# Opening of a two-layer kernel: a third output block in the wide banks, sums of squares by stationary squares, inputs from two queues

## The reference

```
h = rmsnorm(x, g_pre_mix)          # x * rsqrt(mean(x*x) + eps) * g
z = h @ w_in                       # split into s5 input u, conv x/b/c, q, k, v, f, gates
s5_mixer(u, ...), short conv, forgetting attention on q, k, v with decay from f
out = x + rmsnorm((sum of gate * branch @ w_branch) @ w_out, g_post_mix)
```

## Time and profile before

| | |
|---|---|
| median of 3 runs | 3633.23 us (3633.01 to 3633.37) |
| the profiled execution | 3627.11 us, its span 3625.6 us |
| PE busy | 3472.5 us, 96% of the span |
| DVE, ACT, POOL busy | 39%, 24%, 25% |
| mean granted TensorE clock | 0.986 |
| DMA | 333.40 MB, 92 GB/s over the span |

### The profile page before, as it was taken

The page is one execution under the profiler, slowest core; times in us unless marked ns, Lnnn a source line. Parts: engine busy times, 40 slices in busy tenths (PEclk is TensorE's granted clock), DMA queues, the critical chain, the costliest instruction groups (busy, mean ns, idle before and its releaser), DMA issues. The chain is left out here.

```text
span 3625.6 us, 40637 instructions
## 1 busy us (share of the span) xinstructions
PE 3472.5 (96%) x16148; PEld 2802.7 (77%) x16148; DVE 1429.7 (39%) x1581; ACT 874.9 (24%) x1067; POOL 905.2 (25%) x455
## 2 busy tenths in 40 slices
PE   7999999998999999999999999899999899999997
PEld 5787788887876888888867877677777688888886
DVE  7733566554324121212244436553542521121123
ACT  3222222224332111111222222212342411111112
POOL 2211111112331222222421124131254222222224
PEclk9999999999999999999999999999999999999998
DMA  3535434215412111111234222113263211111113
GB/s 120 149 95 140 142 127 136 96 70 198 162 41 76 52 46 47 46 52 46 93 111 126 86 93 93 64 64 135 93 215 127 76 46 46 46 46 52 46 46 128
DMA packets 101600, 333.40 MB, mean 92 GB/s; under 512 B 11920, under 2 KB 21520, under 8 KB 101328
## 3 DMA queue, kind: packets, MB, share of 16 engines
q1 hardware_dynamic: 100000, 326.90, 27.3%
q10 hardware_dynamic: 1472, 4.72, 0.3%
HBM read 249.06 MB, written 85.52 MB: 92 GB/s over the span
## 5 line engine op out<-in xcount | busy, mean ns | idle before, releaser
L272 POOL TENSOR_TENSOR w_lo<-w_raw,w_hi 128x1024 fp32r<-128x1024 f32 (+1 forms) x305 | 691.9, 2272 | 2547.6 <-ACT w_hi L268 2547.3
L311 PE MATMUL pair<-act_hi,w_hi 128*128 128x512 f32 x2992 | 967.4, 404 | 13.8 <-issue 7.4
L311 PE MATMUL pair<-act_lo,w_hi 128*128 128x512 f32 x2992 | 943.4, 396 | 0.0
L311 PE MATMUL pair<-act_hi,w_lo 128*128 128x512 f32 x2992 | 942.2, 396 | 0.0
L311 PEld LDWEIGHTS pair<-act_lo,w_hi 128*128 128x128 f32 x2992 | 564.6, 189 | 138.2
L311 PEld LDWEIGHTS pair<-act_hi,w_lo 128*128 128x128 f32 x2992 | 563.4, 188 | 137.7
L311 PEld LDWEIGHTS pair<-act_hi,w_hi 128*128 128x128 f32 x2992 | 545.2, 189 | 133.9 <-issue 15.9
L268 ACT CAST w_hi<-w_raw 128x1024 fp32r<-128x1024 f32 x275 | 288.4, 1049 | 970.7 <-PE pair L311 911.3
L594 DVE TENSOR_TENSOR p<-pair,rs 128x1024 f32<-128x1024 f32 x100 | 122.3, 1223 | 410.9 <-PE pair L311 398.7
L1832 DVE TENSOR_TENSOR f2v<-pair,rs 128x1024 f32<-128x1024 f32 x42 | 51.5, 1225 | 346.5 <-PE pair L311 346.5
L311 PE MATMUL pair<-f1hl,w_hi 128*128 128x512 f32 x480 | 147.8, 389 | 0.0
(11 more groups left out here) (471 smaller groups left out, 3966.9 us busy)
## 6 DMA issues: line engine op xcount, KB each, us to landing
w_raw<-in_stream SPq DMA_DIRECT2D x276, 512.0 KB, 3.6
proj<-p SPq DMA_DIRECT2D x101, 512.0 KB, 2.6
m2g<-proj SPq DMA_DIRECT2D x32, 512.0 KB, 4.6
foxx<-proj SPq DMA_DIRECT2D x32, 256.0 KB, 5.7
m1g<-proj SPq DMA_DIRECT2D x16, 512.0 KB, 3.3
x<-f1y SPq DMA_DIRECT2D x16, 512.0 KB, 2.6
act_lo<-x SPq DMA_DIRECT2D x16, 512.0 KB, 6.7
n1x<-in_x ACTq DMA_DIRECT2D x8, 512.0 KB, 9.1
```

What stands on the lines that cost most here:

```text
L272: last = nc.gpsimd.tensor_tensor(wlo[:, slot, at:at + n], raw[:, slot, at:at + n], whi[:, slot, at:at + n].bitcast(F32), ALU.subtract)
L311: last = nc.tensor.matmul(out_pair[:, h * HALF:(h + 1) * HALF], wt, a[:, h * HALF:(h + 1) * HALF], start=k == 0 and n_pass == 0, stop=k == ...
```

## The change

It acts in the opening, and by it on what is left for the background.

- The two first weight units are fetched without the wait for `s_split`. The loads x0 to x3 stay with ACT, x4 to x7 go to SP, behind the weights. The three S5 constants go to SP, after tile 0.
- A third output block, U1, is made in the opening. Its weights come as a tensor of their own (`third`), loaded by SP, split by ACT (line 1002) and POOL (line 1003) after tile 0, and its products (line 979) go into `wide`, which `row_sums` no longer needs. Third(0) and third(1) stand behind tile 1, third(k) behind tile k.
- The column sums of the squares are taken by `half_sums` in two banks (line 451): the squares are stationary and a column of ones moves, and the sums come out with one token on a partition, so that neither the diagonal nor the reduction is needed. They stand ahead of the last tile, the root's two halves behind them, the spreading (line 473) behind the last tile of F and U0, and third(7) behind that.
- DVE evicts the third block (line 1970) into the buffer of x0, after the four half evictions, and SP stores it.
- The background has 50 blocks instead of 51. The `upto` marks in S5 are lowered by eight tiles.
- Slots, pairs and the buffers of `p` swap their roles from there on, since one unit less has gone through the stream.

```
     def fetch_unit(b, slot):
-        SP.wait_ge(s_split, b + 1)
+        if not (isinstance(b, int) and b < 2):
+            SP.wait_ge(s_split, b + 1)
...
-                arrived = [x_in_sem[k].mark(nc.scalar.dma_start(x[:, k, :], x_in[k])) for k in range(KT)]
-                s5_in.mark(nc.scalar.dma_start(bb[:, 0:2, :, :], t["s5_b"]))
-                s5_in.mark(nc.scalar.dma_start(cc[:], t["s5_c"]))
-                got = s5_in.mark(nc.scalar.dma_start(dg[:], t["s5_d"]))
-                first_split()
+                raw3, hi3, lo3 = (sb(at, "n1w" + n, [P, KT * P], dt) for n, dt in (("r", F32), ("h", F32R), ("l", F32R)))
+                raw3_in = store.mark(SP.dma_start(raw3[:], t["third"]))
+                arrived = [x_in_sem[k].mark((nc.scalar if k < 4 else SP).dma_start(x[:, k, :], x_in[k])) for k in range(KT)]
...
+                def third(k):
+
+                    for half in halves:
+                        for n_pass, (wt, a) in enumerate(((hi3, act_hi), (hi3, act_lo), (lo3, act_hi))):
+                            last = nc.tensor.matmul(wide[:, half], wt[:, k * P:(k + 1) * P], a[:, k, half],
+                                                    start=k == 0 and n_pass == 0, stop=k == KT - 1 and n_pass == 2)
+                    return last
...
+                    if k == 0:
+                        first_split()
...
+                    if k == KT - 1:
+                        sums = [half_sums(bank[h][:], squares[:, halves[h]], True, True, added[k]) for h in range(2)]
+                        roots = [half_root(h, bank[h][:], 1.0 / D, sums[h]) for h in range(2)]
                     PE.after(split)
                     for o in range(2):
                         for h in range(2):
                             first_two.tile(o, h, k)
+                    if k == 0:
+                        a = A.mark(A.after(raw3_in).copy(hi3[:], raw3[:]))
+                        third_ready = G.mark(G.after(a).tensor_tensor(lo3[:], raw3[:], hi3[:].bitcast(F32), ALU.subtract))
+                        for n in range(3):
+                            s5_in.mark(SP.dma_start((bb[:, 0:2, :, :], cc[:], dg[:])[n], (t["s5_b"], t["s5_c"], t["s5_d"])[n]))
+                        got = s5_in.last()
+                    if k == 1:
+                        PE.after(third_ready)
+                        third(0)
+                    if k == KT - 1:
+                        for h in range(2):
+                            spread = half_spread(h, bank[h][:], roots[h])
+                            rs_ready = A.mark(A.after(spread).copy(rs[:, halves[h]], bank[h][:]))
+                    if k:
+                        last = third(k)
                     if 0 < k < KT - 1:
                         for _ in range(3):
                             next(early, None)
-                spread_inv_sqrt(rs, 1.0 / D, row_sums(squares, 0, 1, added[KT - 1]), rows=True)
-                V.after(A.last())
-                for o, evict in enumerate(first_evicts):
+                third_done = PE.mark(last)
+                V.after(rs_ready)
+                for o, evict in enumerate(first_evicts[0:2]):
                     for h in range(2):
                         first_two.evicted(o, h, evict)
                 stored[F_], stored[U_] = outs[0].last(), outs[1].last()
+                stored[U_ + 1] = first_evicts[2](x[:, 0, :], third_done)
...
-            w.upto(KT + 2)
+            w.upto(2)
...
-            w.upto(3 * KT + 1)
+            w.upto(2 * KT + 1)
...
-        rows = rows[2:]
+        rows = rows[3:]
...
-            w.upto(15 * KT + 1)
+            w.upto(14 * KT + 1)
```

More of the change, by code:

```diff
@@ L973, in s5 @@
                 squares, added = sq[:, 0, :], {}
+                halves = [slice(h * HALF, (h + 1) * HALF) for h in range(2)]
+                def third(k):
[4 more added lines that the diff above has]
+                    return last
                 for k in range(KT):
@@ L1937, in evict_u_half, with evict_third @@
                 outs[o].mark(SP.dma_start(s5_u.rearrange("(n p) j m -> n p (j m)", p=P)[0], buf[:, o, :]))
+        def evict_third(staged, ready):
+            v = V.mark(V.after(ready).tensor_tensor(staged.rearrange("p (j m) -> p j m", j=T),
+                                                    wide[:].rearrange("p (m j) -> p j m", j=T),
+                                                    rs[:].rearrange("p (m j) -> p j m", j=T), ALU.mult))
+            SP.wait_ge(*v)
+            return store.mark(SP.dma_start(s5_u.rearrange("(n p) j m -> n p (j m)", p=P)[1], staged))
         first_two = TwoBlocks(KT, act_rhs)
         with Woven(products(0, used["units"], n, n, KT, act_rhs, evict), n * KT, 1) as w:
-            s5(first_two, (evict_row, evict_u_half), w, stored)
-            w.upto(15 * KT + 1)
+            s5(first_two, (evict_row, evict_u_half, evict_third), w, stored)
+            w.upto(14 * KT + 1)
             w.again(FOX_HEADS * 24 + 8, KT)
@@ L1950, in _build @@
                 ops.load(r, mixed1[r], into=8 + r if r < 4 else None, *{0: (weighed, A.last(), stores[1].last()), 9: (normalised, mixed_out)}.get(r, ()))
-            gates = [gates1[:, 0, :], gates1[:, 1, :], buf[:, 1, :]]
-            merging = merge(ops, proj1, GATE1, 3, "b_gate", gates, buf[:, 0, :], [rs[:], rs[:]],
-                            [(stored[GATE1 + 8 * br], outs[1].last()) for br in range(3)],
+            gates = [gates1[:, 0, :], gates1[:, 1, :], buf[:, 0, :]]
+            merging = merge(ops, proj1, GATE1, 3, "b_gate", gates, buf[:, 1, :], [rs[:], rs[:]],
+                            [(stored[GATE1 + 8 * br], outs[0].last()) for br in range(3)],
                             lambda: [s.last() for s in outs], {0: (8, 12)})
@@ L2025, in _stream @@
     conv = [w[row + n:row + n + 1] for n in range(4) for row in (X_, B_, C_)]
-    parts = [_tiles(f), w[U_:X_], w[Q_:F_], *conv, _tiles(w_in[:, n_f + FOX_HEADS:])]
+    parts = [_tiles(f), w[U_:U_ + 1], w[U_ + 2:X_], w[Q_:F_], *conv, _tiles(w_in[:, n_f + FOX_HEADS:])]
     wb = _tiles(x["w_branch"][0])
@@ L2082, in _lay_out @@
         "stream": _stream(x),
+        "third": _units(_tiles(x["w_in"][0][:, (U_ + 1) * P:(U_ + 2) * P]).reshape(KT, P, P))[0],
         "s5_b": by_pair(b), "s5_c": by_pair(c),
```

## The result

| | before | with the change |
|---|---|---|
| median | 3632.91 us (20 runs, 3627.01 to 3634.88) | 3638.2 us (20 runs, 3631.46 to 3641.87) |
| ratio to before | | 1.0017, 95% interval 1.0010 to 1.0024 |
| the profiled execution | 3627.11 us | 3638.36 us |

The change costs 5.3 us where a gain of 9.7 was forecast.

What follows compares the result with a forecast made beforehand. DVE was taken to bound the stretch before the first transposition of constants, PE nearly all the rest. Opening +0.3, background -11.2 and take-back +1.2 sum to -9.7 us: 3623.5 us from the median 3633.23, range 3619.5 to 3629.5.

Steps and rivals of the forecast that it cites:

- Start of PE: In the opening: earlier weight loads let PE start at 11.45 us instead of 14.41, bounds 10.8 and 12.1.
- PE through the opening: PE stays supplied, `act_lo` of tile 1 just ahead of 16.6; first eviction possible at 50.2 us instead of 51.99.
- rival C: DVE's 33.15 us stretch shortens as POOL's splits fall elsewhere, or the opening is PE-bound earlier: 3620.5 us; chance 0.12.
- From there to `fox`: From the first transposition of constants to `fox`: PE bound again with its order unchanged, slow matmuls as before; zero.
- The background, -11.2: 50 background blocks instead of 51: 48 matmuls fewer, one tile ahead of `fox` and seven in it, -11.2 us.
- take-back: In the attention: tiles gone lengthen waits and their moving pattern opens a few new ones, +1.2 us, bounds 0 and +5.
- The prediction's own sign of being wrong: In `fox`: the prediction is wrong if PE's waits there grow by more than 5 us.
- Rival D: In `fox`: gaps on PE lower the clock, once in each of eight heads, 33 us; total 3656 us; chance 0.03.
- Rival A: In `fox`: half of the eight missing tiles turn into waits, gain only 5.3 us: 3627.9 us; chance 0.15.
- B: In the opening: late weights make `act_lo` of tile 1 2 to 3 us late, never recovered: 3626.2 us; chance 0.09.
- E: The change doesn't do what it says; only the spare bank could be missing; chance 0.01.
- A rule on POOL and DVE: In the opening: DVE and POOL lock each other out on SBUF; the third block's split costs DVE up to 2.4 us.

Runs made afterwards that it cites:

- Experiment 2: Changed kernel, with `fox` preparing the next head one step later (n == 5 instead of 4): 3623.92 us, ratio 0.9973.
- experiment 1: Changed kernel, with the eight missing tiles taken out of the S5 mixer instead of the attention: 3624.95 us, ratio 0.9974.
- experiment 3: Kernel before, with eight more background tiles handed out ahead of the attention and so eight fewer in it: 3651.31 us, ratio 1.0052.
- experiments 5 to 8: 5: kernel before, POOL held for key split, 3632.74 us; 6: later preparation there, 3633.72; 7: experiments 1 and 2 together, 3624.6; 8: kernel before, loads and sums, 3628.75.
- the sums alone: Kernel before, with only the new sums by stationary squares ahead of the last tile: 3631.55 us, ratio 0.9997.
- the loads alone: Kernel before, with only the weights fetched without their wait and x loaded from two queues: 3626.54 us, ratio 0.9988.
- experiment 6: Kernel before, with the next head prepared one step later in `fox`: 3633.72 us, ratio 1.0004.

## Why the prediction was wrong

*Start of PE:* forecast 11.45, measured 11.37. Right.

*PE through the opening:* I had `act_lo` of tile 1 just ahead of 16.6; it came late by 1.20 us, at 17.38, with the sums at 44.75 instead of 43.2. First eviction 51.25 instead of 50.2, constants at 56.96 instead of 55.6, first transposition 89.38 instead of 88.8. The term was +0.3 with bounds of -0.9 and +1.5. At the constants it measured +1.7, just outside; DVE's stretch from there to the transposition is 0.8 us shorter than before (rival C's mechanism, in small), so that +0.9 arrives. The number is within its bounds, partly by luck.

*From there to `fox`:* forecast zero, measured -1.3. The first transposition of `fox` comes 1.8 us earlier, and 1.4 of it is the one tile less ahead of it. The forecast took the slow matmuls behind PE's idle time as unchanged; with the change the clock is 1.00 and 0.83 from 80 to 100 us instead of 0.92 and 0.74.

*The background, -11.2:* stands. Experiment 2 shows it: with waits of 11.1 us in `fox` against 10.3, the stage takes 10.9 us less than before.

***The step that failed* is the take-back,** "the pattern of one or two tiles moves along the whole stage and will open a few new ones", +1.2 with bounds of 0 and +5. It measured 17.7 us: 12.1 of waits, 3.6 to 5.1 of clock, and a rest that no row names. The prediction's own sign of being wrong, waits in `fox` growing by more than 5 us, came. The bound came from the waits that the stage already had the earlier trace rows, and this is the wrong yardstick: shifting a pattern doesn't only lengthen old waits, it brings work of other engines, which comes at each block's end, into steps where it was not. What would have shown it was at hand. I compared the order of PE in `fox`, where one tile was missing, and not that of DVE, where an eviction had changed places in seven heads. And the waits of 0.6 us for line 821 said which step has no slack. A DVE instruction of 1.22 us ahead of it, and the split of the keys stretched beside POOL, for which I had a size from the opening (2.36 and 2.82 us for an operation of 1.28), would have given 1 to 2.5 us per head (an estimate from these rows).

*Rival D* had the mechanism, gaps in `fox` and then the clock, "from about three such gaps on". There were four, with three falls. Its price, one fall in each of eight heads, was too high, and its chance of 0.03 too low. *Rival A* had only waits as long as the tiles taken out. *B* came in small: the third weights are cast at 12.73, forecast about 11.2, and `act_lo` of tile 1 comes 1.2 us late instead of 2 to 3. *C* gave the 0.8 us above and not 3. *E* is out: the third block is made.

*A rule on POOL and DVE.* The rows at 477 us show the two engines one behind the other. POOL starts at 477.28 while DVE still has line 715 to 478.35, and takes 3.31 us where it takes 2.37 alone; line 716 starts at 478.38, and ends 1.1 us after POOL's end at 480.59. The rule of the Trainium skill that I weighed (SBUF — State Buffer, section "Who interferes with whom": the one that starts second blocks until the first is done) fits this within 0.15 us: POOL would end at 478.35 + 2.37 = 480.72 and line 716 at 480.59 + 1.22 = 481.81, where the rows have 480.59 and 481.68. I applied it only to the opening. There it did cost something: `act_lo` of tile 1 takes 2.47 us at 14.86, beside the split of the third weights, and at the 1.28 us of the undisturbed tiles it would have been done at 16.14, where PE waits until 17.38.

## What to carry to other kernels

When a change alters how much background work is spread over a periodic foreground, compare the order on every engine that the end of a block triggers, not only on the one that does the background work. Find the foreground's step without slack from its waits, however small, and ask what now falls into it. Work removed from the background can be more than lost again (11.2 us gained, 17.7 lost), and where the block ends fall can be set by hand: eight tiles given out earlier or later decided 13 us in the changed kernel (experiment 1) and 18 in the one before (experiment 3).

## What was not expected of the hardware

- The granted clock fell behind waits of 2.91 to 2.99 us three times, and not behind one of 2.87. The length alone doesn't decide it. In experiment 3 the same four waits stand in the same order (2.99, 2.87, 2.98 and 2.92), and there the clock fell behind the one of 2.87 and not behind the one of 2.92:

```profile
494.21 0.47 PE L785 MATMUL wide<-foxks,foxqh 128*128 128x512 f32 x1 [2.87 <-DVE foxs L821]
626.76 0.47 PE L785 MATMUL wide<-foxks,foxqh 128*128 128x512 f32 x1 [2.92 <-DVE foxs L821]
```

```profile
495.00:498.00 3.00, 3.00 (x13) 2.42 (x11) 2.90 (x5) 0.94 (x1) 0.00 (x0) 0.61 0.71 220
627.00:630.00 3.00, 3.00 (x16) 2.31 (x16) 2.90 (x5) 1.11 (x2) 0.00 (x0) 1.00 0.84 294
```

- Nor does it take 2.9 us. Eight traces have a wait of 2.2 to 2.3 us for `foxvt` between 426 and 436 us. In five (experiments 5 to 8 and the sums alone) the clock is below 1.00 between 430 and 440 us, 0.83 in four of them; in three (the kernel before, the loads alone and experiment 1) it is not. What decides it stays open.
- An eviction from PSUM isn't slowed by POOL: line 595 took 1.205 to 1.226 us in all its 33 places in `fox`, with POOL's split beside it (in seven) or not. The causal add (line 822 before), with both operands in SBUF, takes 0.29 us alone and 1.62 beside POOL at 619.59 us in experiment 6.
